# Seven products of quarters for every second gate-and-up tile of two feed-forward layers

## The chip, the cores and the metric

The kernel runs on one core of a Trainium2 chip. The metric is the device time of one execution in microseconds (us). A core has TensorE (PE, matmuls; PEld is its weight load), VectorE (DVE), ScalarE (ACT), GpSimd (POOL) and SyncE (SP), which issues most loads. Matrices are multiplied in fp32r: a value is rounded into a high part, the rest is its low part, and each product is made of three matmuls (high x high, high x low, low x high).

## The reference

Four blocks follow one another on 512 tokens of width 1024: a conformer convolution layer, an attention layer, and a layer of two gated feed-forwards around a hybrid attention mixer. Only the last two feed-forwards matter here:

```python
def swiglu(h, w_gate, w_up, w_down):
    return (jax.nn.silu(h @ w_gate) * (h @ w_up)) @ w_down
# h: 512 x 1024, w_gate and w_up: 1024 x 2816, w_down: 2816 x 1024
h = swiglu(rms_norm(x, ff1_norm_pre[l]), ff1_w_gate[l], ff1_w_up[l], ff1_w_down[l])
...
h = swiglu(rms_norm(x, ff2_norm_pre[l]), ff2_w_gate[l], ff2_w_up[l], ff2_w_down[l])
```

## The kernel before, in words

All weights come as chunks of 128x1024 floats, 371 in all, through a ring of four slots (`raw`). SyncE loads chunk c into slot c mod 4 as soon as TensorE is done with chunk c-4 (`chunk_done`). ScalarE rounds the chunk into `wH` (L1253, `high`; in the steady state `high_after(c)` rounds chunk c+3 once chunk c is done), GpSimd subtracts to get `wL` (L506, `split`), which raises `low_ready`, and TensorE waits for that count before it starts on the chunk.

The feed-forwards 2 and 3 are those of the reference above. Each has 22 tiles of 128 hidden features. A tile is a gate chunk and an up chunk; `tile_product` (L560) multiplies one chunk with the whole of x, 8 slices of 128 rows, three matmuls of 128x128 by 128x512 each (L556 to L558), 24 matmuls into one PSUM bank. Tiles alternate between banks 4, 5 and 6, 7. ScalarE applies Silu to the gate bank (L1472), VectorE multiplies by the up bank (L1953, `h_made`), ScalarE rounds the result into `hH` (L1475), and VectorE subtracts to get `hL` (L1955, `h_ready`). The first tile of a layer is made in halves of 256 tokens (`first_chunks`), as x becomes ready. All other tiles but the second are in a hardware loop of eleven passes in `ffn`, which exists once for each engine (TensorE L747, ScalarE L1453, VectorE L1936).

The down product (`full_product`, L589 to L591) then takes one chunk after another, 24 matmuls for each, into all eight banks; before it writes banks 4 to 7 it waits for `h_made` (`banks_free`). Its chunk k waits for `h_ready` of tile k.

Each engine works through its own instructions in the order in which they are written. A wait blocks all that stand behind it on that engine.

## Time and profile before

| what | us |
|---|---|
| median of 3 runs (2322.52 to 2325.39) | 2324.6 |
| profiled execution | 2323.89 |
| its span, first to last instruction | 2322.1 |
| TensorE matmuls busy in it | 2289.5 |
| VectorE / ScalarE / GpSimd busy | 895.6 / 944.9 / 927.0 |
| gate and up tiles of feed-forward 2, about | 1276 to 1530 |
| gate and up tiles of feed-forward 3, about | 1944 to 2210 |

Busy time says how long an engine had an instruction in work; matmuls overlap, so that a matmul's record is longer than the distance to the next start, and the distance is what it costs. A row of the timeline gives start, duration, engine, line, operation, output and inputs, and in brackets how long the engine had been idle and what ended that. An instruction that waits for a port counts as busy. Neighbours of one kind may be merged in a row (x2, x3), with the time from the first start to the last end. A row of a group gives, after the count, busy us and mean ns | idle us before it and what ended it, or the minimum, median and maximum in ns and the first and last start.

### The profile page before, as it was taken

The page shows a single profiled execution, that of the slowest core. Times are in us where ns is not written, and L with a number is a line of the kernel's source. Part 1 is how long each engine was busy: PE and PEld are TensorE (multiplying, and loading weights), DVE is VectorE, ACT ScalarE, POOL GpSimd, SP SyncE. Part 2 cuts the span into 40 slices and gives each one's busy share as a digit, 9 for nine tenths or more (in the row PEclk, how much of TensorE's full clock was granted, in tenths as well). Part 3 has the DMA queues.
Part 4 walks back from the last instruction along what each step waited for, and adds up shares of the span by engine and source line. Part 5 has one row for each costly group of instructions (what it writes and reads, how often), then busy time and mean ns, then how long its engine had stood idle before and what let it go on. Part 6 is the DMA issues. An engine that isn't in the chain of part 4 may idle for free.

```text
span 2322.1 us, 30648 instructions
## 1 busy us (share of the span) xinstructions
PE 2289.5 (99%) x11342; PEld 1874.7 (81%) x11342; DVE 895.6 (39%) x1211; ACT 944.9 (41%) x1598; POOL 927.0 (40%) x410
## 2 busy tenths in 40 slices
PE   8999999999999999999999999999999999999998
PEld 6668888888887878888888888888878768888887
DVE  6963544410544533443302322210657953222201
ACT  6665433321555553333313422221545655222222
POOL 6934444444332235444443444444111003444443
PEclk9999999999999999999999999999999999999999
DMA  6623323223221133222222222222421002322222
GB/s 207 194 91 100 113 95 99 96 94 100 73 73 64 55 118 113 96 99 94 95 100 91 91 98 92 99 98 93 162 75 64 28 28 82 99 96 93 100 98 93
DMA packets 64422, 223.68 MB, mean 96 GB/s; under 512 B 7120, under 2 KB 7120, under 8 KB 64336
## 3 DMA queue, kind: packets, MB, share of 16 engines
q1 hardware_dynamic: 60192, 208.30, 27.0%
q10 hardware_dynamic: 4144, 14.16, 1.9%
q8 instruction: 63, 1.03, 0.2%
q14 instruction: 23, 0.19, 0.0%
HBM read 211.88 MB, written 2.10 MB: 92 GB/s over the span
## 4 chain that ended last, share of the span: by engine, by line
PE 86%; DVE 5%; ACT 4%; issue 2%; POOL 1%; DMA 1%; SPq 0%; DVEq 0%; POOLq 0%; ACTq 0%
PE banks L556 18%; PE banks L557 17%; PE banks L558 17%; PE banks L589 9%; PE banks L591 9%; PE banks L590 9%; DVE banks L2003 2%; DMA raw<-ws 1%; PE banks L1053 1%; POOL pool_sum L519 1%; PE banks L604 1%; PE banks L921 1%; PE banks L909 1%; PE banks L932 1%; PE banks L1097 1%
## 5 line engine op out<-in xcount | busy, mean ns | idle before, releaser
L506 POOL TENSOR_TENSOR wL<-raw,wH 128x1024 fp32r<-128x1024 f32 x346 | 845.2, 2445 | 1229.5 <-ACT wH L1253 1229.4
L1253 ACT ACTIVATE wH<-raw 128x1024 fp32r<-128x1024 f32 x371 | 393.7, 1061 | 1092.4 <-PE banks L558 589.0
L556 PE MATMUL banks<-xH,wH 128*128 128x512 f32 (+1 forms) x1976 | 761.9, 386 | 9.7 <-DVE xL L1812 7.4
L557 PE MATMUL banks<-xL,wH 128*128 128x512 f32 (+1 forms) x1976 | 756.4, 383 | 0.0
L558 PE MATMUL banks<-xH,wL 128*128 128x512 f32 (+1 forms) x1976 | 756.3, 383 | 0.0
L556 PEld LDWEIGHTS banks<-xH,wH 128*128 128x128 f32 x1976 | 371.9, 188 | 90.8 <-DVE wL L1817 8.4
L558 PEld LDWEIGHTS banks<-xH,wL 128*128 128x128 f32 x1976 | 371.9, 188 | 73.0
L557 PEld LDWEIGHTS banks<-xL,wH 128*128 128x128 f32 x1976 | 372.0, 188 | 70.7
L589 PE MATMUL banks<-wH,hH 128*128 128x512 f32 x704 | 273.9, 389 | 0.0
L590 PE MATMUL banks<-wH,hL 128*128 128x512 f32 x704 | 273.9, 389 | 0.0
L591 PE MATMUL banks<-wL,hH 128*128 128x512 f32 x704 | 273.9, 389 | 0.0
L1955 DVE TENSOR_TENSOR hL<-tmp,hH 128x512 f32 x88 | 205.5, 2335 | 98.0 <-ACT hH L1475 98.0
L1953 DVE TENSOR_TENSOR tmp<-banks,tmp 128x512 f32<-128x512 f32 x88 | 60.9, 692 | 366.1 <-PE banks L558 354.2
L591 PEld LDWEIGHTS banks<-wL,hH 128*128 128x128 f32 x704 | 132.1, 188 | 27.5
L590 PEld LDWEIGHTS banks<-wH,hL 128*128 128x128 f32 x704 | 132.1, 188 | 27.5
L589 PEld LDWEIGHTS banks<-wH,hH 128*128 128x128 f32 x704 | 132.1, 188 | 27.3
L1946 DVE SCALAR_TENSOR_TENSOR tmp<-banks,par,tmp 128x511 f32<-128x511 f32 x88 | 65.9, 749 | 139.2 <-ACT tmp L1465 132.4
L1870 DVE SCALAR_TENSOR_TENSOR xr<-xr,banks 128x512 f32<-128x512 f32 x32 | 20.6, 680 | 247.7 <-PE banks L591 247.7
L1899 DVE TENSOR_TENSOR banks<-banks,tmp 128x512 f32<-128x512 f32 x24 | 15.5, 693 | 257.9 <-ACT squares L1363 257.5
L589 PE MATMUL banks<-wH,xH 128*128 128x512 f32 x192 | 75.0, 391 | 0.0
L590 PE MATMUL banks<-wH,xL 128*128 128x512 f32 x192 | 74.7, 389 | 0.0
L591 PE MATMUL banks<-wL,xH 128*128 128x512 f32 x192 | 74.7, 389 | 0.0
(272 smaller groups left out, 2167.5 us busy)
## 6 DMA issues: line engine op xcount, KB each, us to landing
raw<-ws SPq DMA_DIRECT2D x371, 512.0 KB, 3.3
shifted<-gpad SPq DMA_DIRECT2D x32, 258.0 KB, 5.1
w1b<-w ACTq DMA_DIRECT2D x8, 512.0 KB, 5.7
tmp<-rows ACTq DMA_DIRECT2D x7, 512.0 KB, 4.4
b_row<-rows ACTq DMA_DIRECT2D x5, 512.0 KB, 3.6
tmp<-xT SPq DMA_DIRECT2D x8, 256.0 KB, 6.3
xr<-xN ACTq DMA_DIRECT2D x4, 512.0 KB, 3.9
out<-xr SPq DMA_DIRECT2D x3, 512.0 KB, 2.6
```

The source lines that it names most:

```text
L506: pool.tensor_tensor(wL[:, j, :], raw[:, j, :], fp(wH[:, j, :]), ALU.subtract).then_inc(low_ready, 1)
L556: pe.matmul(bank, wH[:, slot, cols], rh, start=start, stop=False)
L557: pe.matmul(bank, wH[:, slot, cols], rl, start=False, stop=False)
L558: return pe.matmul(bank, wL[:, slot, cols], rh, start=False, stop=stop)
L589: pe.matmul(bank, rh, wH[:, slot, w], start=start, stop=False)
L590: pe.matmul(bank, rl, wH[:, slot, w], start=False, stop=False)
L591: return pe.matmul(bank, rh, wL[:, slot, w], start=False, stop=stop)
L1253: act.activation(wH[:, c % SLOTS, :], raw[:, c % SLOTS, :], ACT.Copy).then_inc(high_ready, 1)
L1946: dve.scalar_tensor_tensor(tmp[:, j, back:S], ps[4 + 2 * j][:, 0:S - back], pc(f"fcw{inst}", f * FCONV_W + tap), tmp[:, j, back:S], ALU.mu ...
L1953: dve.tensor_tensor(tmp[:, 2 + j, :], ps[5 + 2 * j][:], tmp[:, j, :], ALU.mult).then_inc(h_made, 1)
L1955: dve.tensor_tensor(hL[:, bass.ds(f, 1), :].rearrange("p o t -> p (o t)"), tmp[:, 2 + j, :], fp(hH[:, bass.ds(f, 1), :].rearrange("p o t - ...
L2003: ins = dve.scalar_tensor_tensor(sums[i % 2], g, w, sums[i % 2], ALU.mult, ALU.add)
```

## The change

From tile 4 on, each odd tile (nine in each of the two layers) is made by Winograd's form of Strassen's scheme. Gate and up weights are stacked, the rows of x are halved (4 slices of 128 each) and the tokens are halved (256 each): eight products of quarters become seven, each of 4 x 3 = 12 matmuls with 256 columns. The even tiles stay as they were, always in banks 4 and 5 now.

- The sums of quarters of x (`wholeX`, `sumX`), rounded and split, are made once per layer by VectorE and ScalarE during tiles 0 to 3.
- The sums of quarters of the weights are made for each seven tile: VectorE adds four times (S1, the second chunk's first half in place, S2, S3), ScalarE rounds two chunks and three sums, and of the five low parts VectorE makes three (first chunk, S2, S1) and GpSimd two (second chunk, S3). GpSimd also splits the two chunks of the next plain tile.
- The order on TensorE is P1 (first chunk, first half), P2 (S2), P3 (second chunk, first half), P4 (S1), P5 (first chunk, second half, on top of P1), P6 (S3), P7 (second chunk, second half). P1 releases nothing; the slot of the first chunk is released by P5 and that of the second by P7.
- VectorE forms the four quarters of the result out of banks 4 to 7; the gate's two halves get their Silu from ScalarE in pieces.
- The whole h lies where `hL` will be. It is rounded and split in pairs of tiles after the loop (the first pair in its last pass). `hH` shares its memory with the mixed weights and mixed x.
- The down product waits for all 24 counts of `h_made` before it writes banks 4 to 7.

The diff, cut to its core; the new `high_h` and `low_h` are in it, and `product` is the twelve matmuls of one product:

```diff
+SEVEN_FROM = 4
+SEVENS = (FT - SEVEN_FROM) // 2
+QH = KT // 2
+MIX_S1, MIX_S2, MIX_S3 = 1, 0, 2
...
+        mixW, mixXH, mixXL = overlay([("mixW", [P, 3, 2, S], F32R), ("mixXH", [P, 4, QH, S // 2], F32R),
+                                      ("mixXL", [P, 4, QH, S // 2], F32R)])
+        sumW, wholeX, sumX = overlay([("sumW", [P, 3, 2, S], F32), ("wholeX", [P, 4, QH, S // 2], F32),
+                                      ("sumX", [P, 4, QH, S // 2], F32)])
+        _, hW = overlay([("hgap", [P, FT, S], F32), ("hW", [P, FT, S], F32)])
...
+            def plain_splits(inst):
+
+                c = CHUNK[f"gateup{inst}"] + 2 * SEVEN_FROM + 2
+                s1 = (c + 1) % SLOTS
+                u = seven_at(inst, 0)
+                with pool.Fori(0, SEVENS) as t:
+                    pool.wait_ge(w_mixed, t * 4 + (4 * u + 3))
+                    pool.wait_ge(high_ready, t * 4 + (c + 2))
+                    pool.tensor_tensor(wL[:, s1, :], raw[:, s1, :], fp(wH[:, s1, :]), ALU.subtract).then_inc(late_low, 1)
+                    pool.wait_ge(w_mix_high, t * 3 + (3 * u + 3))
+                    pool.tensor_tensor(mixW[:, MIX_S3, 1, :], sumW[:, MIX_S3, 1, :], fp(mixW[:, MIX_S3, 0, :]),
+                                       ALU.subtract).then_inc(late_low, 1)
+                    for i in (c + 2, c + 3):
+                        pool.wait_ge(high_ready, t * SLOTS + (i + 1))
+                        pool.tensor_tensor(wL[:, i % SLOTS, :], raw[:, i % SLOTS, :], fp(wH[:, i % SLOTS, :]), ALU.subtract)\
+                            .then_inc(low_ready, 1)
+                return CHUNK[f"down{inst}"] + 2
...
+            splits(2 * KT + SLOTS, CHUNK["gateup2"] + 2 * SEVEN_FROM + 2)
+            splits(plain_splits(2), lo)
...
+            def seven_products(inst, t):
+
+                u = seven_at(inst, 0)
+                s0, s1 = ((CHUNK[f"gateup{inst}"] + 2 * SEVEN_FROM + 2 + i) % SLOTS for i in range(2))
+
+                def product(out, w_h, w_l, x_h, x_l, start=False):
+                    for k in range(QH):
+                        m = slice(k * P, k * P + P)
+                        pe.matmul(out, w_h[:, m], x_h[:, k, :], start=start and k == 0, stop=False, skip_group_check=True)
+                        pe.matmul(out, w_h[:, m], x_l[:, k, :], start=False, stop=False, skip_group_check=True)
+                        mm = pe.matmul(out, w_l[:, m], x_h[:, k, :], start=False, stop=False, skip_group_check=True)
+                    return mm
...
+                pe.wait_ge(h_made, t * 2 + (24 * inst + SEVEN_FROM + 2))
+                pe.wait_ge(x_mixed, 12 * (inst - 1))
+                pe.sem_inc(low_ready, 2)
+                pe.wait_ge(seven_low, t * 3 + (3 * u + 1))
+                product(half_bank(6), *of_chunk(s0, 0), *of_x(0), start=True).then_inc(product_done, 1)
+                pe.wait_ge(seven_low, t * 3 + (3 * u + 2))
+                product(half_bank(7), *mixed_w(MIX_S2), *mixed_x(1), start=True).then_inc(product_done, 1)
+                pe.wait_ge(late_low, t * 2 + (2 * u + 1))
+                pe.wait_ge(h_made, t * 2 + (24 * inst + SEVEN_FROM + 3))
+                product(half_bank(4), *of_chunk(s1, 0), *mixed_x(0), start=True).then_inc(product_done, 1)
+                pe.wait_ge(seven_low, t * 3 + (3 * u + 3))
+                product(half_bank(5), *mixed_w(MIX_S1), *mixed_x(2), start=True).then_inc(product_done, 1)
+                pe.wait_ge(first_kept, t + (u + 1))
+                product(half_bank(6), *of_chunk(s0, 1), *of_x(1)).then_inc(chunk_done, 1)
+                pe.wait_ge(late_low, t * 2 + (2 * u + 2))
+                pe.wait_ge(seven_sum, t * 5 + (5 * u + 2))
+                product(half_bank(4), *mixed_w(MIX_S3), *last_x()).then_inc(product_done, 1)
+                pe.wait_ge(seven_sum, t * 5 + (5 * u + 3))
+                product(half_bank(5), *of_chunk(s1, 1), *mixed_x(3)).then_inc(chunk_done, 1)
+                pe.wait_ge(seven_sum, t * 5 + (5 * u + 4))
...
+                    with pe.Fori(0, SEVENS) as t:
+                        pe.wait_ge(h_made, t * 2 + (24 * inst + SEVEN_FROM + 1))
+                        tile_product(ps[4][:], t * 4 + cp, cp % SLOTS)
+                        pe.wait_ge(h_made, t * 2 + (24 * inst + SEVEN_FROM + 2))
+                        tile_product(ps[5][:], t * 4 + (cp + 1), (cp + 1) % SLOTS)
+                        seven_products(inst, t)
...
-                        pe.wait_ge(h_made, 24 * inst + 21 + q)
+                        pe.wait_ge(h_made, 24 * inst + (21 + q if inst < 2 else 24))
...
+                    if f == 1:
+                        for i, n in ((0, 3), (1, 6), (2, 6), (3, 8)):
+                            act.wait_ge(x_mixed, 12 * (inst - 2) + n)
+                            act.activation(mixXH[:, i, :, :], sumX[:, i, :, :], ACT.Copy).then_inc(x_mix_high, 1)
...
+                def seven_highs(t):
+
+                    high(cs, t)
+                    act.wait_ge(w_mixed, t * 4 + (4 * u + 2))
+                    high(cs + 1, t)
+                    act.wait_ge(w_mixed, t * 4 + (4 * u + 3))
+                    high_mixed(MIX_S2, t)
+                    high_mixed(MIX_S1, t)
+                    act.wait_ge(chunk_done, t * 4 + (cp + 1))
+                    act.wait_ge(h_made, t * 2 + (24 * inst + SEVEN_FROM + 1))
+                    act.activation(tmp[:, 0, :], ps[4][:], ACT.Silu).then_inc(gate_act, 1)
+                    act.wait_ge(w_mixed, t * 4 + (4 * u + 4))
+                    high_mixed(MIX_S3, t)
...
+                def seven_gates(t, last=False):
+
+                    high(cp + 4, t)
+                    act.wait_ge(product_done, t * 5 + (5 * u + 1))
+                    act.activation(tmp[:, 3, HALF[0]], half_bank(6), ACT.Copy).then_inc(first_kept, 1)
+                    high(cp + 5, t)
+                    act.wait_ge(chunk_done, t * 4 + (cs + 1))
+                    act.activation(tmp[:, 1, HALF[0]], half_bank(6), ACT.Silu).then_inc(seven_gate, 1)
+                    if last:
+                        high_h(0)
+                        high_h(2)
+                    act.wait_ge(seven_sum, t * 5 + (5 * u + 4))
+                    act.activation(tmp[:, 1, HALF[1]], tmp[:, 1, HALF[1]], ACT.Silu).then_inc(seven_gate, 1)
+
+                def high_h(f):
+                    act.activation(hH[:, f:f + 2, :], hW[:, f:f + 2, :], ACT.Copy).then_inc(h_high, 2)
...
+                high(d0 + 2)
+                act.wait_ge(product_done, 5 * seven_at(inst, SEVENS))
+                high_h(4)
+                act.wait_ge(chunk_done, d0)
+                for f in range(6, FT, 2):
+                    act.wait_ge(h_made, 24 * inst + 2 + f + 2)
+                    high_h(f)
+                highs(f"down{inst}")
...
+                dve.wait_ge(x_ready, XV[xname] + 2 * KT)
+                joined(2, 0, 1)
+                joined(0, 0, 0)
+                dve.wait_ge(x_mixed, mixed + 2)
+                mix_x(0, whole_x(0), whole_x(2), ALU.subtract)
+                joined(1, 1, 1)
+                plain_first(0)
...
+                    dve.tensor_tensor(sums[MIX_S1], a11, a21, ALU.add).then_inc(w_mixed, 1)
+                    dve.wait_ge(w_mixed, t * 4 + (4 * u + 1))
+                    dve.tensor_tensor(a21, a21, a22, ALU.add).then_inc(w_mixed, 1)
+                    dve.wait_ge(w_mixed, t * 4 + (4 * u + 2))
+                    dve.tensor_tensor(sums[MIX_S2], a21, a11, ALU.add).then_inc(w_mixed, 1)
+                    dve.wait_ge(w_mixed, t * 4 + (4 * u + 3))
+                    dve.tensor_tensor(sums[MIX_S3], sums[MIX_S2], a12, ALU.add).then_inc(w_mixed, 1)
+
+                    def low_slot(s, c):
+                        dve.wait_ge(high_ready, t * 4 + (c + 1))
+                        dve.tensor_tensor(wL[:, s, :], raw[:, s, :], fp(wH[:, s, :]), ALU.subtract).then_inc(seven_low, 1)
+
+                    def low_mixed(n, made):
+                        dve.wait_ge(w_mix_high, t * 3 + (3 * u + made))
+                        dve.tensor_tensor(mixW[:, n, 1, :], sums[n], fp(mixW[:, n, 0, :]), ALU.subtract).then_inc(seven_low, 1)
+
+                    dve.wait_ge(w_mixed, t * 4 + (4 * u + 4))
+                    low_slot(s0, cs)
+                    low_mixed(MIX_S2, 1)
+                    low_mixed(MIX_S1, 2)
...
+                def plain_h(t):
+                    dve.wait_ge(gate_act, t + (plain_gates(inst) + SEVEN_FROM + 1))
+                    dve.wait_ge(chunk_done, t * 4 + (cp + 2))
+                    dve.tensor_tensor(whole_h(t * 2 + SEVEN_FROM), ps[5][:], tmp[:, 0, :], ALU.mult).then_inc(h_made, 1)
+
+                def seven_h(t, last=False):
+
+                    f = t * 2 + (SEVEN_FROM + 1)
+                    h = whole_h(f)
+                    kept, w = tmp[:, 3, HALF[0]], tmp[:, 3, HALF[1]]
+                    dve.wait_ge(first_kept, t + (u + 1))
+                    dve.wait_ge(product_done, t * 5 + (5 * u + 2))
+                    dve.tensor_tensor(w, half_bank(7), kept, ALU.subtract).then_inc(seven_sum, 1)
+                    dve.wait_ge(product_done, t * 5 + (5 * u + 3))
+                    dve.wait_ge(seven_sum, t * 5 + (5 * u + 1))
+                    dve.tensor_tensor(kept, w, half_bank(4), ALU.subtract).then_inc(seven_sum, 1)
+                    dve.wait_ge(product_done, t * 5 + (5 * u + 4))
+                    dve.wait_ge(seven_sum, t * 5 + (5 * u + 2))
+                    dve.tensor_tensor(h[:, HALF[1]], half_bank(5), kept, ALU.add).then_inc(seven_sum, 1)
+                    dve.wait_ge(product_done, t * 5 + (5 * u + 5))
+                    dve.tensor_tensor(tmp[:, 1, HALF[1]], half_bank(4), w, ALU.subtract).then_inc(seven_sum, 1)
+                    if last:
+                        low_h(0)
+                    dve.wait_ge(chunk_done, t * 4 + (cs + 2))
+                    dve.tensor_tensor(h[:, HALF[0]], half_bank(5), w, ALU.add).then_inc(seven_sum, 1)
+                    dve.wait_ge(seven_sum, t * 5 + (5 * u + 5))
+                    dve.wait_ge(seven_gate, t * 2 + (2 * u + 2))
+                    dve.tensor_tensor(h, h, tmp[:, 1, :], ALU.mult).then_inc(h_made, 1)
+
+                def low_h(f):
+                    dve.wait_ge(h_high, FT * inst + f + 2)
+                    dve.tensor_tensor(hL[:, f:f + 2, :], hW[:, f:f + 2, :], fp(hH[:, f:f + 2, :]), ALU.subtract)\
+                        .then_inc(h_ready, 2)
```

## Rows read from the trace of the kernel before

**Rows 1.** the page: span, busy time, and the granted clock in 40 slices

```profile
span 2322.1 us, 30648 instructions
...
PE 2289.5 (99%) x11342; PEld 1874.7 (81%) x11342; DVE 895.6 (39%) x1211; ACT 944.9 (41%) x1598; POOL 927.0 (40%) x410
...
PEclk9999999999999999999999999999999999999999
```

**Rows 2.** the page: the chain that ended last, by engine

```profile
PE 86%; DVE 5%; ACT 4%; issue 2%; POOL 1%; DMA 1%; SPq 0%; DVEq 0%; POOLq 0%; ACTq 0%
```

**Rows 3.** busy time of each engine in two windows; columns as named

```profile
core 0: us, PE busy (x) PEld busy (x) DVE busy (x) ACT busy (x) POOL busy (x), PEclk, DMA share, GB/s
1293.00:1520.00 227.00, 227.00 (x1003) 187.96 (x1002) 63.68 (x42) 66.81 (x86) 102.97 (x43) 1.00 0.30 100
1975.00:2210.00 235.00, 235.00 (x1038) 194.62 (x1037) 63.84 (x43) 66.31 (x84) 105.08 (x44) 1.00 0.29 97
```

**Rows 4.** timeline of TensorE, 512 columns, first and last of 57

```profile
1309.74 0.39 PE L556 MATMUL banks<-xH,wH 128*128 128x512 f32 x1
...
1322.43 0.39 PE L558 MATMUL banks<-xH,wL 128*128 128x512 f32 x1
```

**Rows 5.** timeline of TensorE, 256 columns: first starts, and the next form

```profile
1286.85 0.39 PE L556 MATMUL banks<-xH,wH 128*128 128x256 f32 x1
1287.08 0.28 PE L557 MATMUL banks<-xL,wH 128*128 128x256 f32 x1
...
1292.71 0.40 PE L556 MATMUL banks<-xH,wH 128*128 128x512 f32 x1
```

**Rows 6.** timeline of a chunk's hand-over; loads of L464 to landing

```profile
1303.62 0.39 PE L556 MATMUL banks<-xH,wH 128*128 128x512 f32 x1
...
1303.95 0.33 SPq L464 DMA_DIRECT2D raw<-ws  x1
...
DMA to landing us min/median/max: 3.0/3.2/3.5
```

**Rows 7.** VectorE: an undisturbed subtraction; timeline of a dependent operation

```profile
L1812 DVE TENSOR_TENSOR xL<-tmp,xH x8: 681/684/693, 6.6 to 13.4; 128x512 fp32r<-128x512 f32 x8
...
257.42 0.75 DVE L1946 SCALAR_TENSOR_TENSOR tmp<-banks,par,tmp 128x511 f32<-128x511 f32 x1 [1.27 <-ACT tmp L1465]
258.34 0.75 DVE L1946 SCALAR_TENSOR_TENSOR tmp<-banks,par,tmp 128x510 f32<-128x510 f32 x1 [0.17 <-DVE tmp L1946]
```

**Rows 8.** groups of ScalarE by form, and a split alone in the timeline

```profile
L1253 ACT ACTIVATE wH<-raw 128x1024 fp32r<-128x1024 f32 x371 | 393.7, 1061 | 1092.4 <-PE banks L558 589.0 <-PE banks L591 436.6 <-DMA raw<-ws 66.4
...
L1475 ACT ACTIVATE hH<-tmp 128x512 f32 x88 | 54.1, 614 | 0.5 <-DVE tmp L1953 0.4
...
1354.00 2.40 POOL L506 TENSOR_TENSOR wL<-raw,wH 128x1024 fp32r<-128x1024 f32 x1 [3.13 <-ACT wH L1253]
```

**Rows 9.** VectorE's low part of h: all 88, and one beside a split

```profile
L1955 DVE TENSOR_TENSOR hL<-tmp,hH x88: 1870/2346/2356, 261.9 to 2197.9; 128x512 f32 x88
...
1304.96 2.40 POOL L506 TENSOR_TENSOR wL<-raw,wH 128x1024 fp32r<-128x1024 f32 x1 [2.05 <-ACT wH L1253]
...
1305.57 2.33 DVE L1955 TENSOR_TENSOR hL<-tmp,hH 128x512 f32 x1 [1.06 <-ACT hH L1475]
```

**Rows 10.** timeline: tensor_tensor operations in a row beside a split

```profile
204.08 1.21 DVE L1885 TENSOR_TENSOR xr<-tmp,b_row 128x1024 f32<-128x1024 f32 x1
204.12 6.84 POOL L506 TENSOR_TENSOR wL<-raw,wH 128x1024 fp32r<-128x1024 f32 x1 [1.46 <-ACT wH L1253]
...
205.21 3.49 DVE L1885 TENSOR_TENSOR xr<-tmp,b_row 128x1024 f32<-128x1024 f32 x3
...
870.16 2.35 DVE L1885 TENSOR_TENSOR xr<-tmp,b_row 128x1024 f32<-128x1024 f32 x2
870.20 6.84 POOL L506 TENSOR_TENSOR wL<-raw,wH 128x1024 fp32r<-128x1024 f32 x1 [1.46 <-ACT wH L1253]
```

**Rows 11.** timeline: scalar_tensor_tensor ahead of tensor_tensor, beside a split

```profile
245.86 1.22 DVE L1932 SCALAR_TENSOR_TENSOR xr<-xr,tmp 128x1024 f32<-128x1024 f32 x1
247.00 3.41 DVE L1930 TENSOR_TENSOR tmp<-tmp,proj 128x1024 f32<-128x1024 f32 x1
...
246.07 3.26 POOL L506 TENSOR_TENSOR wL<-raw,wH 128x1024 fp32r<-128x1024 f32 x1 [3.88 <-ACT wH L1253]
```

**Rows 12.** groups by form: other prices; GpSimd at 512 behind VectorE

```profile
L2200 DVE TENSOR_TENSOR wL<-raw,wH x23: 1216/1226/2026, 1664.4 to 1818.0; 128x1024 fp32r<-128x1024 f32 x23
...
L1953 DVE TENSOR_TENSOR tmp<-banks,tmp 128x512 f32<-128x512 f32 x88 | 60.9, 692 | 366.1 <-PE banks L558 354.2 <-ACT tmp L1472 9.9 <-ACT tmp L1469 2.0
...
L1913 DVE SCALAR_TENSOR_TENSOR xL<-banks,par,xH x96: 472/474/484, 195.2 to 1963.8; 128x256 fp32r<-128x256 f32 x96
...
L1556 ACT ACTIVATE banks<-banks 128x256 f32<-128x256 f32 x16 | 5.7, 429 | 0.0
...
1677.87 1.22 DVE L2200 TENSOR_TENSOR wL<-raw,wH 128x1024 fp32r<-128x1024 f32 x1
...
1678.35 1.88 POOL L542 TENSOR_TENSOR ksL<-cosine,ksH 128x512 fp32r<-128x512 f32 x1 [20.80 <-ACT ksH L1679]
```

More of the change, by code:

```diff
@@ L521, in splits @@
             def splits(lo, hi):
-                with pool.Fori(lo // SLOTS, hi // SLOTS) as t:
+                up, down = -(-lo // SLOTS) * SLOTS, hi // SLOTS * SLOTS
+                for c in range(lo, up):
+                    split(c // SLOTS, c % SLOTS)
+                with pool.Fori(up // SLOTS, down // SLOTS) as t:
                     for j in range(SLOTS):
                         split(t, j)
+                for c in range(down, hi):
+                    split(c // SLOTS, c % SLOTS)
+            def plain_splits(inst):
[14 more added lines that the diff above has]
+                return CHUNK[f"down{inst}"] + 2
             pool.wait_ge(low_ready, 2)
@@ L535, in _ @@
             lo, hi = hybrid0 + LEAD, hybrid0 + LEAD + NITEMS
-            splits(2 * KT + SLOTS, lo // SLOTS * SLOTS)
-            for c in range(lo // SLOTS * SLOTS, lo):
-                split(c // SLOTS, c % SLOTS)
+            splits(2 * KT + SLOTS, CHUNK["gateup2"] + 2 * SEVEN_FROM + 2)
+            splits(plain_splits(2), lo)
             for i in ROPES:
@@ L543, in _ @@
             pool.wait_ge(low_ready, hi)
-            for c in range(hi, -(-hi // SLOTS) * SLOTS):
-                split(c // SLOTS, c % SLOTS)
-            splits(-(-hi // SLOTS) * SLOTS, NCHUNKS // SLOTS * SLOTS)
-            for j in range(NCHUNKS % SLOTS):
-                split(NCHUNKS // SLOTS, j)
+            splits(hi, CHUNK["gateup3"] + 2 * SEVEN_FROM + 2)
+            splits(plain_splits(3), NCHUNKS)
         @block.tensor
@@ L1643, in _ @@
             halve_row("ff1_post")
-            ffn(2)
+            seven_ffn(2)
             post_and_pre("down2", "mix_pre", "hybrid")
@@ L1803, in _ @@
             halve_row("ff2_post")
-            ffn(3)
+            seven_ffn(3)
             for q in range(QT):
```

122 lines of the change are left out of this document (116 added, 6 removed).

## The prediction

> **What bounds the kernel now.** I read the page first, then the chain, then the matmuls of the two stretches that change. TensorE is busy 99% of the span, every other engine 39 to 41%, and the granted clock is at its upper level, 2.4 GHz, in every slice [rows 1]; 86% of the chain that ended last is TensorE's [rows 2]. In the gate and up products of the two last feed-forward layers TensorE is busy for the whole of both windows [rows 3]. So the change is worth what it takes from TensorE's stream, less what its new waits put into it. The page's mean of 386 ns for a matmul is no price: matmuls overlap, and what one costs is the distance between starts. With 512 columns, 57 matmuls start between 1309.74 and 1322.43: 12.69 / 56 = 0.2266 us each [rows 4]. With 256 columns, the form that the change brings, 47 start from 1287.08 on until the next matmul at 1292.71: 5.63 / 47 = 0.1198 us each [rows 5]. Half the columns costs 53% of the time, and that decides the size of the gain.
>
> **TensorE's sum.** A tile is now two chunks of 24 matmuls, 48 x 0.2266 = 10.88 us, and this is also the rhythm at which the other engines are seen to work (a chunk every 5.44 us). A seven-product tile has 7 x 12 = 84 matmuls of 256 columns: 84 x 0.1198 = 10.06 us. The arithmetic falls by an eighth, the time by 0.81 us, 7.5%, because 36 more matmuls each bring the fixed part. Nine tiles in each of two layers: 18 x 0.81 = 14.7 us.
>
> The Trainium skill (TensorE: Matmul & The Clock Gate, Back-to-back issue gap) gives an isolated spacing of N/2.4 + 2.5 ns. By it the tile would save 48 x 215.8 - 84 x 109.2 ns = 1.19 us, 21 us in all, an estimate. The rows show about 13 ns above N/2.4 at both sizes, with a weight load ahead of each matmul; the measured spacing is used.
>
> **What has to be ready, and when.** Let 0 be the moment when the last product of the previous seven tile hands TensorE to the plain tile; the next product P1 is due at 10.88, P2 at 12.32, P3 at 13.76, P4 at 15.19 (12 x 0.1198 = 1.44 us each), P5 to P7 to 20.94. Before, only 66 us of the 1092 us that ScalarE idled ahead of its chunk roundings ended on a load [rows 8]; the others waited for TensorE. Now the second weight chunk of the seven tile is released only at 0, and everything derived from it has 10.9 to 15 us.
>
> - The load. A matmul's record ends 0.16 us after the next one may start; SyncE issued 0.33 us after such a handover (1303.62 to 1303.95), and landing takes 3.2 us (3.0 to 3.5) [rows 6]. Landed at about 3.55.
> - VectorE's four additions of 128x512, both inputs in SBUF. Nearest row: 684 ns for the same shape undisturbed; an operation that waits for the one in front starts 0.17 us after its end [rows 7]. Four in a chain: 3.55 to 6.81.
> - ScalarE rounds the changed chunk after the second sum, 5.2 to 6.3 (1.06 us), then S2 and S1 (0.61 each), the plain tile's Silu, and S3 by about 8.1 [rows 8].
> - GpSimd could take the low part of that chunk from 6.36. Alone it is 2.40 us [rows 8]. But GpSimd and a VectorE operation with two SBUF inputs do not run together: the 512-wide subtraction in the feed-forward loop takes 2346 ns where it would need 0.68, since it starts 0.6 us into a GpSimd split and ends 0.54 us after it [rows 9]. So the split starts with the end of the fourth addition, 6.81, and ends 2.25 us later at 9.06.
> - VectorE's low part of the first chunk (1.22 us undisturbed [rows 12], 1.08 after a release) is issued at 6.98 and ends at 10.14. P1 has 0.7 us to spare.
>
> Then two low parts of 128x512 (S2, S1) and the plain tile's gate times up (0.69 us, one operand in PSUM, not disturbed) stand in this order on VectorE, and P3 waits for the last. On GpSimd stand S3's low part (1.14 us after a release [rows 12], taken as 1.16), which waits from 9.06, and the split of the next plain chunk (2.25 us), whose load and rounding are done by 10.3. Who has the port between two VectorE operations that follow without a gap decides the outcome. Four VectorE tensor_tensor operations of 128x1024 held GpSimd off for all four: its split was issued at 204.12, the first of them at 204.08, and it took 6.84 us, 4.6 of them waiting; the same at 870.20 [rows 10]. Where the leading operation is a scalar_tensor_tensor it was otherwise: GpSimd, issued at 246.07, went in at the boundary near 247.08, and the VectorE operation of 247.00 took 3.41 us [rows 11]. The change's run is tensor_tensor throughout, as in rows 10, so I take it that VectorE keeps the port from 9.06 on: low parts ready at 10.14, 10.77 and 11.39, plain product at 12.02 for a due time of 13.76. GpSimd then does S3 to 12.55 (due 18.07), the next two splits to 14.95 and 17.98 (due 20.94 and 26.4). No product waits.
>
> The Trainium skill (SBUF — State Buffer, SBUF: two separate sides) calls this port pair an exclusive lock for a whole instruction, and the one that starts first has it. Rows 9 agree (2346 ns); by the rule alone each end of an operation opens the port, which is the second rival below, and rows 10 speak against it.
>
> **Smaller terms.** The differences and sums between products (five of 128x256 on VectorE, one operand in PSUM; the nearest rows are 474 ns for another operation at that width and 0.69 at double) and the 256-wide copy and Silus on ScalarE (429 ns) come 0.8 to 3 us ahead of P6, P7 and the next plain tile: nothing, and up to 0.11 us wherever TensorE does stop, since the first spacing after a wait is 0.23 in place of 0.12 (1286.85 to 1287.08) [rows 5, 12]. The mixing of x ahead of the loop (12 VectorE operations of 1.22 us, 4 ScalarE ones of 1.06) lies beside four plain tiles of 10.9 us, where VectorE was busy 64 of 227 us [rows 3]: nothing; if it were late, once per layer at most 3 us. SyncE's queue issues the same loads in the same order; two of four come later, and DMA is at 0.3 of its share [rows 3]: nothing. TensorE's own increment of the split counter and some ten more waits an iteration: bounds 0 and 0.11 at each of seven product starts; the chunk starts in the loop, with their waits, show no wider spacing [rows 4], so I take 0. The rounding and low parts of h move behind the loop. The last iteration's first pair is subtracted only after the sum that follows P6, at 20.1 to 21.3, so the down product starts about 0.5 us late, in two layers: +1.0 us; bounds 0 and 3. The other ten pairs (1.22 us, 3.4 with a blocked port) are needed one every 10.9 us: nothing.
>
> Sum: -14.7 + 1.0 = -13.7 us. On the profiled execution (span 2322.1, execution 2323.9, 1.8 us around it) that is 2310.2; the median of the runs is 0.7 above that execution, so 2310.9. I predict 2311 us. Its own range, from no start-up loss to bubbles at half of the product starts, is 2308 to 2318.
>
> **Rivals.**
> 1. *GpSimd gets in between VectorE's low parts* (place: the boundary at 10.14; it decides once the port is yielded between back-to-back tensor_tensor operations, as in rows 11 and not in rows 10). S3 runs 10.14 to 11.30, S2's low part to 11.85, the next split to 14.10, S1's low part to 14.64, the plain product to 15.27, P3 at 15.4 instead of 13.76: 1.63 us an iteration against a saving of 0.81. 18 x 0.82 + 1 = +15.8: 2340 us, slower. A load 0.3 us sooner would give 2335.
> 2. *GpSimd also keeps the port at its own boundaries*: S3 and the next split go ahead of the first low part, which then ends at 13.85, P1 3.1 us late: 18 x (3.1 - 0.8) + 1 = +42, 2367 us. Against it: in rows 10 the later splits ran only once VectorE was done, which leaves it open; in rows 11 VectorE's waiting operation went as soon as GpSimd ended.
> 3. *The saving is eaten by TensorE's restarts*: 0.11 us at each of seven product starts, 18 x 0.77 = 13.9 us: 2325 us, no change. For it: seven waits against computed counts, one after another; against it rows 4.
>
> **How the numbers follow.** Forecast 0.55, rival 1 0.27, rival 2 0.04, rival 3 0.10, mixed outcomes (some iterations blocked) 0.04. No change means within 0.2%, 4.6 us, about what a measurement of this kernel can tell. Faster: the forecast, nearly all of its range, and part of rival 3 and the mixed ones, 0.60; same 0.11; slower 0.29. The range goes from 2306 (spacing 2% better, no loss at the end) to 2341, which takes in rival 1 and leaves rival 2 and the worse half of rival 1's spread out.
>
> **What would show it.** Right: 256-column matmuls of the seven products 0.12 us apart with no gap at product starts; a loop iteration of 20.9 us against 21.8; VectorE's two 512-wide low parts in about 0.65 us each right behind the 1024-wide one; a GpSimd S3 record of over 3 us, most of it waiting. Wrong: TensorE waiting for VectorE's gate-times-up product (rival 1) or for its 1024-wide low part (rival 2), VectorE low parts of 1.8 and 2.9 us, an iteration of 22.6 or 24; spacings of 0.23 at every product start (rival 3). A load landing over 0.7 us later than 3.55 would make P1 wait even if the port is kept.

## The result, and the profile after

Medians of 7 runs of each kernel: the changed one 2333.55 us (2332.99 to 2335.45), the kernel before 2324.6 (2322.33 to 2325.9). The ratio of after to before is 1.0041, 95% interval 1.0029 to 1.0053: slower by 0.3 to 0.5%, where 2311 us had been forecast. The profiled execution's span is 2332.2 us against 2322.1.

The page of the changed kernel, for [rows 1] and [rows 2]: its span, busy time by engine, and the chain that ended last.

```profile
span 2332.2 us, 32552 instructions
...
PE 2278.4 (98%) x11990; PEld 1893.0 (81%) x11990; DVE 1101.4 (47%) x1429; ACT 990.5 (42%) x1674; POOL 943.7 (40%) x410
...
PEclk9999999999999999999999999999999999999999
...
PE 75%; DVE 10%; issue 6%; ACT 5%; DMA 4%; POOL 1%; DVEq 0%; SPq 0%; ACTq 0%; POOLq 0%
```

TensorE has 11 us less to do at the same clock, and the span is longer. Its part of the chain fell from 86% to 75%, and VectorE's doubled from 5 to 10%. The two stretches of [rows 3] show the same thing (the busy time in windows; columns as there):

```profile
1297.00:1525.00 228.00, 218.73 (x1311) 195.09 (x1310) 142.38 (x136) 79.52 (x113) 106.30 (x42) 1.00 0.27 94
1979.00:2206.00 227.00, 216.57 (x1301) 193.10 (x1300) 140.40 (x136) 78.36 (x112) 103.20 (x41) 1.00 0.27 94
```

TensorE, which was busy for the whole of both windows, now has holes of 9.3 and 10.4 us. TensorE's waits (who waited for what: total us, times, longest us) name the operation, and the timeline shows where the hole lies:

```profile
PE banks L814 <- DVE hW L2211: 19.4, 18, 1.7
...
PE banks L648 <- DVE hL L2239: 0.6, 2, 0.3
```

```profile
1338.34 0.28 PE L815 MATMUL banks<-mixXL,mixW 128*128 128x256 f32 x1
1338.46 0.28 PE L816 MATMUL banks<-mixXH,mixW 128*128 128x256 f32 x1
1339.72 0.39 PE L814 MATMUL banks<-mixXH,wH 128*128 128x256 f32 x1 [0.98 <-DVE hW L2211]
1339.95 0.28 PE L815 MATMUL banks<-mixXL,wH 128*128 128x256 f32 x1
1340.07 0.28 PE L816 MATMUL banks<-mixXH,wL 128*128 128x256 f32 x1
```

The first matmul of P3 (L814) waits, in all 18 seven-product tiles, for VectorE's gate times up of the plain tile (L2211, the old L1953). In the rows P2's last matmul starts at 1338.46, P3's first at 1339.72 and its second at 1339.95. Without a stop these would be 0.12 apart twice, so the stop costs 1.49 - 0.24 = 1.25 us, 0.27 of it beyond the wait that is listed. The other product starts stand 0.12 behind the matmul in front, but for P1, which follows a matmul of 512 columns by 0.23; one P2, in the pass whose load came last, lost 0.1 us more. Why L2211 is late shows in the lines of VectorE and GpSimd, here of the next pass (TensorE went over to its plain tile at 1347.02):

```profile
1350.67 0.69 DVE L2187 TENSOR_TENSOR sumW<-raw 128x512 f32<-128x512 f32 x1 [2.11 <-DMA raw<-ws]
1351.39 0.69 DVE L2189 TENSOR_TENSOR raw<-raw 128x512 f32<-128x512 f32 x1
...
1352.85 0.69 DVE L2193 TENSOR_TENSOR sumW<-sumW,raw 128x512 f32<-128x512 f32 x1
1353.66 3.22 DVE L2197 TENSOR_TENSOR wL<-raw,wH 128x1024 fp32r<-128x1024 f32 x1
1356.81 4.58 DVE L2201 TENSOR_TENSOR mixW<-sumW,mixW 128x512 fp32r<-128x512 f32 x2
1361.31 0.68 DVE L2211 TENSOR_TENSOR hW<-banks,tmp 128x512 f32 x1
```

```profile
1353.26 2.54 POOL L579 TENSOR_TENSOR wL<-raw,wH 128x1024 fp32r<-128x1024 f32 x1 [10.40 <-ACT wH L1374]
1355.76 2.27 POOL L581 TENSOR_TENSOR mixW<-sumW,mixW 128x512 fp32r<-128x512 f32 x1
1357.99 2.85 POOL L585 TENSOR_TENSOR wL<-raw,wH 128x1024 fp32r<-128x1024 f32 x1
```

The two engines take turns. GpSimd's first split runs to 1355.80, then VectorE's first low part to 1356.88, then GpSimd's S3 (L581: 2.27 us in its record, half of it waiting, where the forecast had over 3) to 1358.03, then S2's low part, then GpSimd's split of the next plain chunk (L585) to 1360.84, and only then S1's. The two low parts of 128x512, forecast at 0.65 us each, take 4.58 together. That is rival 1, operation by operation, and it is so in all 18 passes: S2's low part takes 1.77 to 1.78 us and S1's 2.87 to 2.90, where the prediction gave 1.8 and 2.9 as rival 1's sign.

Sum against the profiled execution: 18 stops at P3, 19.4 us of listed wait and 18 x 0.27 = 4.9 around them; 2 x 0.46 = 0.9 us at the start of the down products; the saving of 14.7 us. 19.4 + 4.9 + 0.9 - 14.7 = +10.5, against a measured span of +10.1 (the medians of the runs differ by 9.0).

### The profile page after: what moved, and what is told of

It is laid out like the page before. It is cut to its first block, busy times and chain, and to the rows that moved or that the text cites. A ratio compares the mean times of both kernels' runs of the same rounds, so it can differ in the third digit from the quotient of the medians.

```text
span 2332.2 us, 32552 instructions
## 1 busy us (share of the span) xinstructions
PE 2278.4 (98%) x11990; PEld 1893.0 (81%) x11990; DVE 1101.4 (47%) x1429; ACT 990.5 (42%) x1674; POOL 943.7 (40%) x410
## 4 chain that ended last, share of the span: by engine, by line
PE 75%; DVE 10%; issue 6%; ACT 5%; DMA 4%; POOL 1%; DVEq 0%; SPq 0%; ACTq 0%; POOLq 0%
PE banks L615 12%; PE banks L617 12%; PE banks L616 12%; PE banks L648 9%; PE banks L649 9%; PE banks L650 9%; DMA raw<-ws 4%; DVE mixW L2201 2%; PE banks L814 2%; PE banks L816 2%; PE banks L815 2%; DVE banks L2319 2%; PE banks L1174 1%; POOL pool_sum L558 1%; PE banks L663 1%
## 5 line engine op out<-in xcount | busy, mean ns | idle before, releaser
L545 POOL TENSOR_TENSOR wL<-raw,wH 128x1024 fp32r<-128x1024 f32 x274 | 682.5, 2494 | 1005.8 <-ACT wH L1374 1005.7
L615 PE MATMUL banks<-xH,wH 128*128 128x512 f32 (+1 forms) x1688 | 650.0, 385 | 9.4 <-DVE xL L2004 7.2
L616 PE MATMUL banks<-xL,wH 128*128 128x512 f32 (+1 forms) x1688 | 644.4, 382 | 0.0
L617 PE MATMUL banks<-xH,wL 128*128 128x512 f32 (+1 forms) x1688 | 644.2, 382 | 0.0
L615 PEld LDWEIGHTS banks<-xH,wH 128*128 128x128 f32 x1688 | 317.8, 188 | 78.7 <-DVE wL L2009 8.1
L617 PEld LDWEIGHTS banks<-xH,wL 128*128 128x128 f32 x1688 | 317.8, 188 | 61.7
L616 PEld LDWEIGHTS banks<-xL,wH 128*128 128x128 f32 x1688 | 318.0, 188 | 59.1
L2271 DVE TENSOR_TENSOR hL<-tmp,hH 128x512 f32 x44 | 102.8, 2336 | 47.3 <-ACT hH L1667 47.3
L579 POOL TENSOR_TENSOR wL<-raw,wH 128x1024 fp32r<-128x1024 f32 x18 | 45.1, 2506 | 184.7 <-ACT wH L1374 184.7
L585 POOL TENSOR_TENSOR wL<-raw,wH 128x1024 fp32r<-128x1024 f32 x36 | 94.6, 2628 | 32.6 <-ACT wH L1374 32.6
L2201 DVE TENSOR_TENSOR mixW<-sumW,mixW 128x512 fp32r<-128x512 f32 x36 | 82.6, 2331 | 0.0
```

Source lines behind the costliest of these rows:

```text
L545: pool.tensor_tensor(wL[:, j, :], raw[:, j, :], fp(wH[:, j, :]), ALU.subtract).then_inc(low_ready, 1)
L585: pool.tensor_tensor(wL[:, i % SLOTS, :], raw[:, i % SLOTS, :], fp(wH[:, i % SLOTS, :]), ALU.subtract)\
L615: pe.matmul(bank, wH[:, slot, cols], rh, start=start, stop=False)
L616: pe.matmul(bank, wH[:, slot, cols], rl, start=False, stop=False)
L617: return pe.matmul(bank, wL[:, slot, cols], rh, start=False, stop=stop)
L2201: dve.tensor_tensor(mixW[:, n, 1, :], sums[n], fp(mixW[:, n, 0, :]), ALU.subtract).then_inc(seven_low, 1)
```

## The experiments

Theory: what costs some 1.3 us a tile is the order in which the shared port is granted, with the plain product last in VectorE's queue. Rivals: the wait in front of P3 is only where lateness from elsewhere shows, or the seven products cost more than their 0.12 us a matmul. The kernel before was at 2322.15 us (2322.08 to 2325.22) beside the first four kernels; spans are compared with the 2322.1 us of the profiled execution above.

### The plain product before the last low part

```diff
-                    low_mixed(MIX_S1, 2)
+                    return lambda: low_mixed(MIX_S1, 2)
...
-                    mix_weights(t)
+                    low_s1 = mix_weights(t)
                     plain_h(t)
+                    low_s1()
...
```

> The changed kernel with one edit: on VectorE the plain tile's gate times up stands ahead of S1's low part instead of behind it. Theory A (the port: GpSimd gets in between VectorE's low parts, and only the plain product behind them comes too late): the wait of P3 for it, 1.1 us in each of 18 passes plus 0.11 for the restart, goes; S1's low part, up to 14.6 us after the hand-over, is still ahead of P4 at 15.2. A pass of 20.9 us, about 2310 us, ratio to the kernel before 0.994. Theory B (the chain from the late second chunk is too long as a whole, the plain product is only where it shows): the wait turns up in front of P4 behind S1's low part; half of the gain or less, 2322 or more, ratio 0.999 or above.

2310.15 us, ratio 0.9945 (0.9929 to 0.9962), span 2308.7. VectorE and GpSimd in its timeline:

```profile
1352.65 3.22 DVE L2197 TENSOR_TENSOR wL<-raw,wH 128x1024 fp32r<-128x1024 f32 x1
1355.79 1.78 DVE L2201 TENSOR_TENSOR mixW<-sumW,mixW 128x512 fp32r<-128x512 f32 x1
1357.49 0.68 DVE L2211 TENSOR_TENSOR hW<-banks,tmp 128x512 f32 x1
1358.09 2.29 DVE L2201 TENSOR_TENSOR mixW<-sumW,mixW 128x512 fp32r<-128x512 f32 x1
```

```profile
1354.74 2.28 POOL L581 TENSOR_TENSOR mixW<-sumW,mixW 128x512 fp32r<-128x512 f32 x1
1356.98 2.85 POOL L585 TENSOR_TENSOR wL<-raw,wH 128x1024 fp32r<-128x1024 f32 x1
```

The port is as contested as before: the two low parts still take 1.78 and 2.29 us. But the product, which reads one operand from PSUM, runs in 0.68 us beside GpSimd's split, and the low part that comes last is due a product later. No wait of TensorE in the two loops is left. Moving one VectorE operation past another turns +10 us into -13.4 us of span, where -13.7 had been forecast; by the medians it is -12.0, beside runs of the kernel before that spread over 3 us. Within that, the stop was the whole of the error.

### GpSimd held back

```diff
+                    pool.wait_ge(h_made, t * 2 + (24 * inst + SEVEN_FROM + 3))
                     for i in (c + 2, c + 3):
```

> The changed kernel with one edit: GpSimd waits with the splits of the next plain tile's two chunks until VectorE has made the plain tile's gate times up. Theory A (the port): the split that goes in between S2's and S1's low parts is what delays the product by about 2.3 us; without it the product is ready some 1 us before P3 is due, no wait is left, the splits end near 16 and 18.5 us for due times of 20.9 and 26.4: 2310 us, ratio 0.994. Theory B (the chain as a whole, with GpSimd's two low parts in it, is too long): P3 still waits, 2325 or more.

2311.41 us, ratio 0.995 (0.9933 to 0.9966), span 2309.9:

```profile
1357.94 2.38 DVE L2202 TENSOR_TENSOR mixW<-sumW,mixW 128x512 fp32r<-128x512 f32 x2
1360.24 0.68 DVE L2212 TENSOR_TENSOR hW<-banks,tmp 128x512 f32 x1
```

With only S3 left to get in between, the two low parts take 2.38 us in place of 4.58. It is the split of the next plain chunk that made P3 late; S3 alone is covered. One of the 18 passes still stopped, for some 0.5 us ahead of P1 and P2: its load came 4.8 us after the hand-over (1347.01 to 1351.80).

### P3 waits for the bank, not for the product

```diff
-                pe.wait_ge(h_made, t * 2 + (24 * inst + SEVEN_FROM + 3))
+                pe.wait_ge(gate_act, t + (plain_gates(inst) + SEVEN_FROM + 1))
                 product(half_bank(4), *of_chunk(s1, 0), *mixed_x(0), start=True).then_inc(product_done, 1)
                 pe.wait_ge(seven_low, t * 3 + (3 * u + 3))
+                pe.wait_ge(h_made, t * 2 + (24 * inst + SEVEN_FROM + 3))
```

P3 writes bank 4, which is free once the Silu has read it; the product reads bank 5, which P4 writes.

> The changed kernel with one edit on TensorE: P3, which writes the bank that only the Silu reads, waits for the Silu; P4, which writes the other bank, waits for the plain tile's gate times up. The order of work on VectorE and GpSimd is untouched, and so is the collision. Theory A: the product, ready at about 15.0 us, is just ahead of P4 at 15.2: no wait or one of up to 0.3 us, 2310 to 2316, ratio 0.994 to 0.996. Theory B (another input of P3 or P4 is as late): half of the gain or less, 2322 or more.

2309.76 us, ratio 0.9944 (0.9927 to 0.9961), span 2309.3. The low parts still take 4.58 us:

```profile
1355.56 4.58 DVE L2202 TENSOR_TENSOR mixW<-sumW,mixW 128x512 fp32r<-128x512 f32 x2
1360.07 0.68 DVE L2212 TENSOR_TENSOR hW<-banks,tmp 128x512 f32 x1
```

So nothing has to run faster; the wait stood one product, 1.44 us, earlier than the data asks. Here too one pass of the 18 stopped, at P1, P2 and P4, for 1.0 us in all, its load being in 4.75 us after the hand-over (2013.75 to 2018.50). The margin is thin: the prediction's closing remark, that a load over 0.7 us later than 3.55 would make P1 wait, came true in these two passes.

### All five low parts on VectorE

The two operations leave GpSimd's loop. The second chunk's low part goes between those of S2 and S1, S3's behind the plain product.

```diff
                     low_mixed(MIX_S2, 1)
+                    dve.wait_ge(high_ready, t * 4 + (cs + 2))
+                    dve.tensor_tensor(wL[:, s1, :], raw[:, s1, :], fp(wH[:, s1, :]), ALU.subtract).then_inc(late_low, 1)
                     low_mixed(MIX_S1, 2)
...
```

> The changed kernel with the second half of the change undone: all five low parts on VectorE (first chunk, S2, second chunk, S1, then the plain product, then S3), GpSimd has only its splits. Theory A (collisions of the two engines cost the time, not VectorE's own work): nothing holds the port while VectorE makes four low parts in about 3.7 us, they end near 10.3, just as the next split is ready, the plain product at 11.8: no wait, 2310 us, ratio 0.994. Theory C (VectorE is too slow for five low parts, which is why two were given away): P1 or P2 waits, VectorE's part before P3 grows by 1.2 us and the time stays at 2330 or rises.

2310.56 us, ratio 0.9951 (0.9934 to 0.9967), span 2307.4. VectorE, and GpSimd's next split:

```profile
1351.59 1.23 DVE L2191 TENSOR_TENSOR wL<-raw,wH 128x1024 fp32r<-128x1024 f32 x1
1352.73 0.69 DVE L2195 TENSOR_TENSOR mixW<-sumW,mixW 128x512 fp32r<-128x512 f32 x1
1353.33 1.22 DVE L2201 TENSOR_TENSOR wL<-raw,wH 128x1024 fp32r<-128x1024 f32 x1
1354.47 0.69 DVE L2195 TENSOR_TENSOR mixW<-sumW,mixW 128x512 fp32r<-128x512 f32 x1
1356.24 0.69 DVE L2207 TENSOR_TENSOR hW<-banks,tmp 128x512 f32 x1 [1.08 <-PE banks L611]
```

```profile
1355.14 2.39 POOL L579 TENSOR_TENSOR wL<-raw,wH 128x1024 fp32r<-128x1024 f32 x1 [12.91 <-ACT wH L1368]
```

VectorE has two more operations, one of them in this run and S3's behind the product, and the run of low parts ends 3.57 us after it began (1351.59 to 1355.16), where with GpSimd's help it took 7.73 (1353.66 to 1361.39). VectorE then waits 1.08 us for TensorE's up product, and P3 begins at 1358.77, 1.84 us after the plain product's end: it no longer waits. Both fixes together (all low parts on VectorE, and P3 waiting for the Silu):

> All five low parts on VectorE (as in the run before) and TensorE's two waits each on its own bank (as in the run before). Theory A: both alone leave no wait in the loop, so together nothing more is to be had: 2309 to 2311, ratio 0.994 to 0.995. If a rest of waiting was hidden in each, up to 2 us less.

2310.22 us against 2322.88, ratio 0.9945 (0.9928 to 0.9962), span 2309.3: nothing is left there to be had.

### Who gets the port: by itself

A kernel that only copies x to the output, and between this has 12 stretches in which VectorE does four operations without a gap while GpSimd, issued 0.07 to 0.14 or 0.28 to 0.35 us behind the first, does two of 128x1024. Kinds: tensor_tensor, the same to fp32r, with waits, scalar_tensor_tensor, half width, mixed.

> Computes nothing of the reference: x is copied to the output, and beside it twelve stretches run in which VectorE makes four operations of 128x1024 (in one pair of stretches 128x512) with two SBUF inputs back to back, and GpSimd two subtractions of 128x1024 that are released about 0.1 or 0.5 us after VectorE's first. Kinds, each at both distances: tensor_tensor with fp32 output, with fp32r output, the same with a wait ahead of each, scalar_tensor_tensor, 512 wide, and both operations in turn. Theory A1 (the port goes to whoever waits at each boundary, whatever the operation): in all twelve GpSimd's first record is 3.2 to 3.5 us, VectorE's second 3.4, and the two engines alternate. Theory A2 (the kind of operation or of output decides, as rows 10 and 11 seemed to show): tensor_tensor with fp32 output holds GpSimd off for all four, 6.8 us, and the fp32r and scalar_tensor_tensor forms do not. Theory A3 (the distance decides: a request that comes within 0.1 us of the start of VectorE's first is not seen until the run ends): 6.8 us at the short distance in all kinds, 3.2 at the long one.

In all 12 the port changes hands at each end of an operation while the other engine wants it. Four operations of 128x1024 take 8.92 us in place of some 4.6. The mixed stretch:

```profile
103.89 1.23 DVE L89 SCALAR_TENSOR_TENSOR dout<-da,db 128x1024 f32<-128x1024 f32 x1 [0.69 <-ACT ab L63]
105.03 3.36 DVE L87 TENSOR_TENSOR dout<-da,db 128x1024 f32<-128x1024 f32 x1
108.32 3.36 DVE L89 SCALAR_TENSOR_TENSOR dout<-da,db 128x1024 f32<-128x1024 f32 x1
111.60 1.21 DVE L87 TENSOR_TENSOR dout<-da,db 128x1024 f32<-128x1024 f32 x1
```

The kind that leads doesn't matter. This takes away the distinction between [rows 10] and [rows 11] on which the forecast stood. The second kernel (x only copied again) tries the distance, from GpSimd 0.11 us ahead to 0.43 us behind, in 14 of 20 stretches with two PSUM-reading operations in front, as in [rows 10]:

> Computes nothing of the reference: x is copied to the output. Twenty stretches in which VectorE makes four tensor_tensor operations of 128x1024 back to back, with two SBUF inputs, and GpSimd two subtractions. In 14 of them VectorE runs two operations that read PSUM just ahead, as in rows 10; the distance between VectorE's first and GpSimd's release goes in steps of 0.04 us from about 0.1 before to 0.4 after. In 6, one small operation stands ahead. Theory A1 (alternation always): GpSimd's first record is never above 3.6 us. Theory A3 (a request that comes within some 0.05 us of the start of VectorE's first is held off until the run of VectorE's operations ends): 6.8 us in the one or two stretches where the distance is 0.02 to 0.06 us, 3.2 to 3.5 in the others. If neither shows 6.8, rows 10 stay unexplained.

All 20 take turns. [rows 10] have a distance of 0.04 us; the nearest stretches have 0.03 and 0.07. The one at 0.03:

```profile
42.39 4.49 DVE L87 TENSOR_TENSOR dout<-da,db 128x1024 f32<-128x1024 f32 x2
```

```profile
42.42 3.39 POOL L56 TENSOR_TENSOR pout<-pa,pb 128x1024 fp32r<-128x1024 f32 x1 [3.23 <-ACT ad L70]
```

Last, [rows 10] in their own place, with the kind changed and with the operands exchanged (one run each, 2322.93 and 2323.84 us beside 2323.47):

```diff
-                dve.tensor_tensor(xr[:, q, :], xg[:, q, :], b_row[:], ALU.add).then_inc(res_step, 1)
+                dve.scalar_tensor_tensor(xr[:, q, :], xg[:, q, :], 1.0, b_row[:], ALU.mult, ALU.add).then_inc(res_step, 1)
```

> The kernel before, with one operation changed in kind: the additions 1024 columns wide at L1885 (four in a row on VectorE, beside which a split of GpSimd was held off until the fourth had ended, its record 6.84 us) are written as scalar_tensor_tensor with a factor of 1.0. Everything else stays. Theory A (a tensor_tensor followed by a tensor_tensor doesn't let GpSimd in at this place, a scalar_tensor_tensor does): the split's record there falls from 6.84 to some 3.3 us and the last of the four additions ends some 2 us later. Theory B (the place, not the kind, decides: what GpSimd or VectorE did just before): the record stays at 6.84 us. The time of the kernel stays within 0.2% of the kernel before under both, as it is two stretches of a few us outside the last feed-forward layers.

> The kernel before, with the two operands of the same additions at L1885 exchanged, kind and order unchanged. Theory A (kind decides) and theory B (the place decides) both expect the split's record beside them to stay at 6.84 us. Theory C (which operand is read first decides whether GpSimd gets in between two additions): it falls to some 3.3 us. The kernel's time stays within 0.2% of the kernel before under all three.

The split's record is 6.84 us in both, at both places, and in every changed version of the kernel too. With the kind changed:

```profile
203.13 3.49 DVE L1885 SCALAR_TENSOR_TENSOR xr<-tmp,b_row 128x1024 f32<-128x1024 f32 x3
203.17 6.84 POOL L506 TENSOR_TENSOR wL<-raw,wH 128x1024 fp32r<-128x1024 f32 x1 [1.47 <-ACT wH L1253]
```

Theory B's expectation is what came, but it says only that the place decides. It is not the only place. In the kernel with ten seven-product tiles (next section), in feed-forward 3, a split came 0.15 us after the start of one of VectorE's low parts of h behind the loop, and was let in only behind the third, when VectorE had no more to do:

```profile
2211.10 5.75 DVE L2240 TENSOR_TENSOR hL<-hW,hH 128x1024 fp32r<-128x1024 f32 x5
2213.52 5.58 POOL L545 TENSOR_TENSOR wL<-raw,wH 128x1024 fp32r<-128x1024 f32 x1 [6.83 <-ACT wH L1374]
```

The same happens there at 2200.17 when all low parts are on VectorE. In the other 16 runs of these low parts in the kernels of this document the split came 0.09 to 0.24 us before the start of the next of them and went in at that boundary, and turns followed, as in the changed kernel (split at 2216.77):

```profile
2216.99 3.43 DVE L2239 TENSOR_TENSOR hL<-hW,hH 128x1024 fp32r<-128x1024 f32 x1
```

So the moment of the request within VectorE's run may matter, but in the 32 stretches, where the request came up to 0.43 us into VectorE's first operation, GpSimd was let in all the same. What lets VectorE keep the port at these places stays open.

### Ten tiles in place of 18

Does the loss go with the count of seven-product tiles? `SEVEN_FROM` 12 leaves five a layer. First as changed, then with all low parts on VectorE.

```diff
-SEVEN_FROM = 4
+SEVEN_FROM = 12
...
-                plain_first(3)
+                for f in range(3, SEVEN_FROM):
+                    plain_first(f)
```

> The changed kernel with seven products for every second tile from tile 12 on instead of 4: 10 of them in the two layers in place of 18. Theory A: each costs a net 0.5 us over a plain tile (1.3 of wait less 0.8 of matmuls), the rest (the end of the layer) is fixed at about 0.6 us: 9 us over before at 18 tiles becomes 5.5 at 10, ratio 1.0024. Theory D (a fixed cost per layer, in mixing x or behind the loop, is the loss, and the tiles gain): the time rises or stays at 9 over, ratio 1.004 or more.

> All five low parts on VectorE, and seven products for every second tile only from tile 12 on: 10 of them. Theory A: without the wait each is worth 0.81 us less 1 us in all for the end of the layers: 18 gave about 12 us, 10 give about 7.5, ratio 0.9968. If the matmul spacing were not what the gain is made of, the gain would not go with the number of tiles.

2330.94 us against 2322.88, ratio 1.0036 (1.0024 to 1.0049), span 2329.1; and 2318.36, ratio 0.998 (0.997 to 0.999), span 2315.7. The second is -6.4 us of span where ten savings of 0.81 and 0.9 at the ends make -7.2. The first was expected at 1.0024, and is slower: its loss against the kernel before is 8.1 us by the medians, where 18 tiles lost 9.0, and its interval takes in the 1.004 from which the rival's expectation began. So the times alone don't show that the loss goes with the count. The waits do:

```profile
PE banks L814 <- DVE hW L2212: 11.7, 10, 1.4
```

11.7 + 10 x 0.27 - 8.1 + 0.9 = +7.2, against +7.0 of span. A stop costs 1.17 + 0.27 = 1.44 us here where it was (19.4 + 4.9) / 18 = 1.35. There are as many stops as tiles, but the size of one goes with the moment at which the load lands. Over the 28 passes of both kernels, the space from P2's last matmul to P3's first is 1.23 us where VectorE's first addition starts 3.52 us after the hand-over, 1.48 at 3.77, 1.67 at 3.94 and 1.99 at 4.42. In feed-forward 2 this kernel's first additions start at 3.79 to 3.94 us, in the changed kernel at 3.52 to 3.65.

### The first pair of h earlier

On top of "all five low parts on VectorE", the first pair of h is rounded after P2 and subtracted ahead of the sum behind P6.

```diff
+                    if last:
+                        act.wait_ge(product_done, t * 5 + (5 * u + 2))
+                        high_h(0)
...
+                    if last:
+                        low_h(0)
                     dve.wait_ge(product_done, t * 5 + (5 * u + 5))
                     dve.tensor_tensor(tmp[:, 1, HALF[1]], half_bank(4), w, ALU.subtract).then_inc(seven_sum, 1)
-                    if last:
-                        low_h(0)
```

> All five low parts on VectorE, and in the last pass of each layer the first pair of h is rounded right after P2 and subtracted ahead of the sum that follows P6, so that it is ready before the down product. Theory A: the 0.47 us gap at the start of the down product goes in both layers, 0.9 us in all: a span of 2306.5, median 2309 to 2310, ratio 0.994 to 0.995; the trace shows whether the gap is gone, the time can't tell 1 us.

2308.52 us against 2324.47, ratio 0.9933 (0.9917 to 0.995), span 2307.1. The wait of L642 for `hL` is gone from the list, and the down product starts 0.12 us behind P7's last matmul, where in the version without it it waited. It is the fastest of all here by its median, but its interval overlaps those of the other five fixed versions. Its span is only 0.3 us below that of the version it builds on, where 0.9 was to be had; but from P1 of the last seven-product tile to the down product it takes 10.07 us in both layers in place of 10.54, so the 0.9 are there, and it had come to the first seven-product tile 0.76 us later (1335.68 against 1334.92).

## Why the prediction was wrong

**The step that failed** is "so I take it that VectorE keeps the port from 9.06 on". It rested on [rows 10], two places, against [rows 11], told apart by the kind of the leading operation. In the loop of the changed kernel GpSimd went in at every boundary, in all 18 passes (VectorE's two low parts took 1.77 and 2.88 us in place of 0.65 each), and so P3 stopped for 1.35 us a tile, 24.3 us in all, that the sum had at nothing. In 32 stretches made for it, of either kind, the port changed hands at every end of an operation, and in [rows 10]'s own place another kind changed nothing. The Trainium skill (SBUF — State Buffer, SBUF: two separate sides) has the port pair as a lock held for one instruction; by that rule alone each end of an operation opens it, and the loop (1.77 and 2.88 us) and the 32 stretches agree, with two open exceptions, [rows 10] and the low parts of h above (5.58 us). (The prediction calls this case "the second rival below"; it is the first of its list.)

**Rival 1's mechanism was right, its price too high.** It had P3 1.63 us late; in the pass shown P3's first matmul starts at 1362.04, 15.02 us after the hand-over at 1347.02 and so 1.26 after its due time of 13.76. Set against the same hand-over, its working reads: additions done at 6.81 (measured 1353.54, which is 6.52), first low part at 10.14 (9.86), S3 at 11.30 (11.01), the split at 14.10 (13.82), S1's low part at 14.64 (14.37), the plain product at 15.27 (14.97). All of it is 0.3 us early, and what made it so is the additions: each was priced with 0.17 us behind the one it depends on, from a scalar_tensor_tensor in [rows 7], and they stand 0.03 to 0.04 apart (1350.67 + 0.69 to 1351.39). The load was taken at 3.55 and the first addition began at 3.65. So 0.1 later, 0.4 sooner. The rest of the difference is P3's start behind the product, 0.13 in the working and 0.05 here. The prediction had said that a load 0.3 us sooner would bring rival 1 to 2335; 2333.55 came.

**TensorE's sum was right.** 256-column matmuls are 0.12 us apart across all product starts but P3. The kernel with all low parts on VectorE has passes of 20.98 us (hand-over to hand-over, 1344.99 to 1365.97), where 10.88 + 10.06 = 20.94 was forecast, and its span is 14.7 us below the 2322.1 of before (its median is 11.6 below the 2322.15 beside it), where the forecast was 13.7. Rival 3 (restarts at each product) and rival 2 (GpSimd's S3 and split both ahead of VectorE's first low part) did not show.

**The end of the layer was right.** The down product starts 0.46 us late in each layer, forecast at 0.5. The mixing of x, the later loads and SyncE's queue cost nothing that shows in TensorE's waits.

**The chances.** Forecast 0.55 against rival 1 at 0.27 was the wrong way round. The case for the forecast was two rows of one place outside the loop; [rows 9], where GpSimd and a 512-wide subtraction meet in the same loop, show who waits, not who is let in. The range to 2341 held the time because rival 1 was worked out.

**What would have made the forecast true** is a change of order: the same arithmetic, with the product one operation earlier, is at 2310.15 us.

## What to carry to other kernels

Where two engines share a port, work out the schedule with turns taken at every end of an operation (what all passes of the loop showed, though two places of these traces did otherwise), and put first in each queue what is due first; handing a fast engine's short operations to a slow one on the same port can lengthen the run that it was to shorten (3.57 us alone, 7.73 with help). An operation that TensorE waits for goes ahead of those that only the next product needs, and a wait belongs in front of the first instruction that touches the bank, not of the group. If a forecast hangs on a rare pattern of the trace, look for a second place that differs in one thing only before trusting it above the common one.

## What the runs showed of the hardware

- A 128x1024 GpSimd split and VectorE operations with both inputs in SBUF took strict turns, whichever kind led: 32 of 32 stretches, four VectorE operations of 128x1024 in 8.92 us, a blocked one 3.36 us for 1.21; and in all 18 passes of the changed loop.
- Two places did not. Four additions held a split off until they had ended (a record of 6.84 us, 4.6 of it waiting), at about 203 and 869 us, in every version of the kernel, also with another kind and with exchanged operands. And in two versions low parts of h held one off for three operations (5.58 us, 3.3 of it waiting). Why is open; distance of issue to VectorE's first operation (0.03 and 0.07 us), PSUM reads ahead and kind are excluded as sole causes.
- A tensor_tensor of VectorE that waited for the one in front started 0.03 to 0.04 us after its end.
- A stop of TensorE cost 0.27 us beyond the listed wait (1.49 us over two starts, less 0.24, less 0.98).
